# Top-k selection rounds spread over the attention's units, and the expert loop written out, in a float32 two-layer decoder trunk

## What is computed

```python
for l in range(2):
    # mixer: one input projection, two causal attentions, gates, output projection
    c_q, c_kv, k_r, dq, dk, dv, iq, ik, iw, gates = split_cols(x @ w_in[l])
    y_a = mla_branch(c_q, c_kv, k_r, pos, ...) @ w_o_mla[l]        # 8 heads
    y_b = dsa_branch(dq, dk, dv, iq, ik, iw, pos) @ w_o_dsa[l]     # 8 heads, 64 best keys per query
    g = sigmoid(gates)
    h = (g[..., :D] * y_a + g[..., D:] * y_b) @ w_out[l]
    x = layer_norm(ALPHA * x + h, ...)
    # layer 0: dense SwiGLU; layer 1: top-2 of 8 experts, D_FF_EXPERT = 3584
    x = layer_norm(ALPHA * x + (swiglu(x) if l == 0 else moe(x)), ...)
```

## Time and profile before

| | |
|---|---|
| median of 3 runs | 1639.26 us (1639.09 to 1640.32) |
| the profiled execution | 1640.06 us |
| its span in the trace | 1638.1 us |
| PE, DVE, ACT busy | 98%, 79%, 63% |
| attention of layer 0, of layer 1 | about 103 to 168 us, 503 to 568 us |
| expert jobs | 644 to 1626 us |
| mean granted TensorE clock | 0.989 of full speed |

### The profile page before, as it was taken

How to read it: one execution, slowest core, us unless ns; L and a number is a source line. 1 busy time by engine, 2 the same in 40 slices (tenths; PEclk the granted TensorE clock), 3 DMA queues, 4 the chain that set the end, 5 groups by cost and what they waited for, 6 DMA issues and landing times.

```text
span 1638.1 us, 20583 instructions
## 1 busy us (share of the span) xinstructions
PE 1601.2 (98%) x7637; PEld 1331.7 (81%) x7638; DVE 1292.3 (79%) x1298; ACT 1024.6 (63%) x947; POOL 55.9 (3%) x54
## 2 busy tenths in 40 slices
PE   8999999999999999999999999999999999999996
PEld 7888788888788788878888888888887888888885
DVE  6794675445697566888989888989888989888887
ACT  4655543443465643776777776777776777777773
POOL 0000000000000001000000200000200000200000
PEclk9999999999999998999999999999999999999998
DMA  9543366555453355899999998999998999999992
GB/s 313 182 146 116 105 217 206 192 187 187 134 172 129 103 181 189 308 357 323 364 376 366 367 373 310 369 375 365 357 375 317 370 375 364 369 372 335 364 371 88
DMA packets 230696, 453.23 MB, mean 277 GB/s; under 512 B 9920, under 2 KB 15552, under 8 KB 230592
## 3 DMA queue, kind: packets, MB, share of 16 engines
q1 hardware_dynamic: 228400, 447.60, 77.4%
q10 hardware_dynamic: 2192, 4.23, 0.7%
HBM read 450.75 MB, written 1.05 MB: 276 GB/s over the span
## 4 chain that ended last, share of the span: by engine, by line
PE 89%; DVE 7%; ACT 2%; issue 1%; DMA 0%; DVEq 0%; SPq 0%; ACTq 0%
PE bank L1515 27%; PE bank L1517 27%; PE bank L1516 27%; PE bank L1990 3%; DVE split L424 2%; PE bank L1685 1%; ACT split L418 1%; DVE split L440 1%; PE bank L1905 1%; ACT split L435 1%; PE bank L1876 0%; PE bank L1877 0%; PE bank L1714 0%; PE bank L1713 0%; DMA raw<-w_in_dram 0%
## 5 line engine op out<-in xcount | busy, mean ns | idle before, releaser
L440 DVE TENSOR_TENSOR split<-raw,split 128x2048 fp32r<-128x2048 f32 x327 | 747.4, 2289 | 110.7 <-ACT split L435 106.6
L435 ACT CAST split<-raw 128x2048 fp32r<-128x2048 f32 x327 | 625.6, 1914 | 188.8 <-PE bank L1517 188.8
L1515 PE MATMUL bank<-split,xe_pair 128*128 128x512 f32 x784 | 310.3, 396 | 3.8 <-DVE split L440 2.2
L1517 PE MATMUL bank<-split,xe_pair 128*128 128x512 f32 x784 | 305.9, 390 | 0.0
L1516 PE MATMUL bank<-split,xe_pair 128*128 128x512 f32 x784 | 305.3, 389 | 0.0
L424 DVE TENSOR_TENSOR split<-raw,split 128x2048 fp32r<-128x2048 f32 (+3 forms) x96 | 208.2, 2175 | 111.3 <-ACT split L418 111.0
L418 ACT CAST split<-raw 128x2048 fp32r<-128x2048 f32 (+3 forms) x96 | 174.3, 1818 | 169.2 <-PE bank L1517 169.2
L1515 PE MATMUL bank<-split,xT 128*128 128x512 f32 (+2 forms) x544 | 218.5, 402 | 4.5 <-DVE split L424 2.4
L1516 PE MATMUL bank<-split,xT 128*128 128x512 f32 (+2 forms) x544 | 209.3, 385 | 0.0
L1517 PE MATMUL bank<-split,xT 128*128 128x512 f32 (+2 forms) x544 | 209.2, 385 | 0.0
L1515 PE MATMUL bank<-split,hT 128*128 128x512 f32 x488 | 190.7, 391 | 0.0
(11 more groups left out here) (246 smaller groups left out, 1620.3 us busy)
## 6 DMA issues: line engine op xcount, KB each, us to landing
raw<-moe_w_dram SPq DMA_DIRECT2D x330, 1024.0 KB, 6.1
raw<-w_in_dram SPq DMA_DIRECT2D x31, 1024.0 KB, 5.1
raw<-dense_w_dram SPq DMA_DIRECT2D x30, 1024.0 KB, 5.0
raw<-w_out_dram SPq DMA_DIRECT2D x8, 1024.0 KB, 5.1
early<-moe_w_dram SPq DMA_DIRECT2D x6, 1024.0 KB, 12.6
raw<-w_o_mla_dram SPq DMA_DIRECT2D x4, 1024.0 KB, 5.1
raw<-w_o_dsa_dram SPq DMA_DIRECT2D x4, 1024.0 KB, 5.2
raw<-w_in_dram SPq DMA_DIRECT2D x4, 912.0 KB, 5.3
```

The costliest lines, as they stand in the source:

```text
L435: act.copy(split[:, n % SPLIT, HEAD, :], landing(n, j)[:, :]).then_inc(heads_made, 1)
L440: dve.tensor_tensor(split[:, n % SPLIT, REST, :], landing(n, j)[:, :], split[:, n % SPLIT, HEAD, :].bitcast(F32), ALU.subtract).then_inc(r ...
L1515: pe.matmul(out_, act_[REST], w[HEAD], start=first, stop=False)
L1517: return pe.matmul(out_, act_[HEAD], w[REST], start=False, stop=last)
```

## The change

In the attention (twice, once for each layer) DVE no longer does rounds 1 and 2 of `best_keys` and the rest of unit 16 ahead of `maxima(0)`. The rest of unit 16 comes behind `maxima(0)`, that of unit 17 behind `maxima(1)`, and one round of `best_keys` behind each of `maxima(0)` to `maxima(6)`; `selection()` follows `maxima(7)` instead of `maxima(6)`. The expert loop is emitted as straight code on all engines, with constants where registers stood. No arithmetic is added or left out.

```diff
         def all_jobs(eng, job):
 
             job(FIRST_JOB, "first")
-            with eng.Fori(1, EXPERTS - 1, 2) as j:
-                job((j, 0), "odd")
-                job((j, 1), "even")
+            for j in range(1, EXPERTS - 1):
+                job((j, 0), "odd" if j % 2 else "even")
             job((EXPERTS - 1, 0), "last")
...
             expert_stream(FIRST_JOB, 0)
-            with sp.Fori(1, EXPERTS - 1, 2) as e:
+            for e in range(1, EXPERTS):
                 expert_stream((e, 0), e)
-                expert_stream((e, 1), e + 1)
-            expert_stream((EXPERTS - 1, 0), EXPERTS - 1)
...
             pair_picks(FIRST_JOB, 1)
-            with pool.Fori(1, EXPERTS - 1, 2) as e:
+            for e in range(1, EXPERTS):
                 weights_of((e, 0), e)
-                weights_of((e, 1), e + 1)
-                pool.wait_ge(comb_tr, nth(1, (e, 1), 1 + CREDIT))
-                pair_picks((e, 1), e + 2)
-            weights_of((EXPERTS - 1, 0), EXPERTS - 1)
+                if e % 2 == 0:
+                    pool.wait_ge(comb_tr, nth(1, (e, 0), 1 + CREDIT))
+                    pair_picks((e, 0), e + 1)
...
                 keys_turned(1)
                 ropes_dsa(1, False)
                 rest(15)
-                rest(16)
-                best_keys(range(1, 3))
...
                 for u in range(16):
                     maxima(u)
-                    if u == 0:
-                        rest(17)
-                    if u < 5:
-                        best_keys(range(3 + u, 4 + u))
+                    if u < 2:
+                        rest(16 + u)
+                    if u < 7:
+                        best_keys(range(1 + u, 2 + u))
                     if u == 4:
                         rest(18)
-                    if u == 6:
+                    if u == 7:
                         selection()
                     if u == 7:
                         rest(19)
```

## The result

The changed kernel takes 1630.86 us, the median of 5 executions (1625.26 to 1631.29), against 1639.26 us before: a ratio of 0.9941, interval 0.9930 to 0.9953. In two later sets of executions it gave 0.9936 and 0.9956. It is faster, by 8.4 us between the medians where 7.9 were forecast (the ratio, which uses all executions, says 9.7, interval 7.7 to 11.5). The two numbers lie close together partly by luck: one term was missing, one came out larger, and the clock gave something that no term had.

What follows compares the result with a forecast made beforehand. PE, busy 98% of the span, was taken as the bound, so only its pauses could go: attention 4.2 plus loop 3.7 is 7.9 us, from 1639.26 to 1631.4 us. The range given was 1629.6 to 1634.8.

Steps and rivals of the forecast that it cites:

- Attention, 4.2 us: `qk(3)` no longer waits for `maxima(1)`, which has 1.5 us to spare; 2.1 us per layer, bounds 3.8 and 4.4.
- The loop, 3.7 us: Starts of jobs 3 and 5: PE's pauses of 1.8 and 1.9 us go, as at job 7.
- upper bound of 4.1: Most that the loop term was said to give; its lower bound was some 2.0 us.
- The rule on branches: Loop: a compare-and-branch costs about 108 ns, so two passes back are worth 0.2 us and the sum 4.4.
- The cost sits in going back: Jobs 3 and 5: the branch taken costs the pause, not the order of work; job 7, not taken, has none.
- I take no change: TensorE's clock behind each attention: same pauses, only earlier, so 0; a stretch more or less is worth 1.7 us.
- Attention gives nothing: Rival, chance 0.09: `maxima(1)` or `maxima(2)` misses its 1.5 us of cover; 1635.6 us, up to 1636.
- the loop gives only what a branch costs: Rival, chance 0.06: code comes late in straight line too, or DVE's order is the cause; 1634.9 us.
- More at half clock: Rival, chance 0.08: shifted pauses bring one or two stretches more, 1633.1 or 1634.8 us; one fewer gives 1629.7.
- more than one stretch: Sign that the forecast is wrong: more than one stretch at the lower clock comes or goes.
- The stalls of fresh straight code: Rival "Slower", chance 0.02: new code for jobs 3 to 6 stalls PE 16 times by 1.8 us; 1660 us.
- The forecast's own range: 1629.7 to 1633.3 us, from the bounds of both terms and one clock stretch; the forecast's chance was 0.72.

Runs made afterwards that it cites:

- experiments on single edits: Changed kernel with only the rests moved (rounds 1 and 2 as before), 1629.82 us; with only the rounds moved (rest of unit 16 as before), 1633.47 us.
- two instructions more: Changed kernel with rounds 1 and 2 ahead of `maxima(0)` as before and both rests moved; executes 19210 instructions in place of 19208; 1629.82 us.
- each half: Kernel before with the attention's edits alone, 1632.32 us (0.9965); changed kernel with the attention as before, so the loop written out alone, 1634.57 us (0.9976).
- padded: Changed kernel with 64 increments of an unused semaphore on DVE in layer 0; 1627.65 us, ratio 0.9927 to the kernel before.
- without the crowded code: Changed kernel without the code for experts with over 128 tokens and the jump over it; 1627.32 us, ratio 0.9926 to the kernel before.
- the last set: Changed kernel, unchanged, run again beside the kernel with 64 more DVE instructions; 1631.04 us, ratio 0.9956 to the kernel before.

## Why the prediction was right, and where it was not

**Attention, 4.2 us.** Right in mechanism: the pause, its cause, its cover (1.5 forecast, 1.7 seen) and the absence of a next one all came as said. From `qk(0)` to `qk(6)` the traces are 2.2 us shorter per layer, 4.3 in all. Half of the reason was idle, though: the text lets the two rounds and the rest go together, and the experiments on single edits show that the rest alone does it.

**The loop, 3.7 us.** The pauses went and jobs 3 and 5 start like job 7. The stage from job 1 to the last experts gave 4.2 to 4.3 us, a little over the upper bound of 4.1: the second matmul of the job was late too, by 0.1 us (1013.79 to 1014.12 in place of 0.23 apart). The engine that the term looked at was only half of it: DVE's own way back costs 3.2 us of stage by itself, hidden behind PE's 4.1. The rule on branches that would have left only 0.2 us (the Trainium skill, "Advanced Engine Details and Errata", Control Flow Timing, about 108 ns) is not borne out: PE idles 1.40 to 1.96 us per pass back, and the measurement decides.

**The step that failed** is that this term ended with the last job. "The cost sits in going back" was taken to mean that only the branches back cost. But straight code also moves everything behind it, and a jump forward at the very end now costs 2.09 us of issue in place of 0.48, 2.0 us in all, uncovered. The loop is thus worth 4.3 - 2.0 = 2.3 us and some 0.2 around the span (the time outside it is 1.72 in place of 1.95), in place of 3.7. The price of a jump whose target's code is late stood in the rows already, at jobs 3 and 5; what was missing was to ask which other jumps the edit would move. DVE's loop kept, jump left out, 64 instructions of padding and two instructions more each make the long pause vanish: this is shown.

**The other step that failed** is "I take no change" for the clock. Over all executions whose clock is on record, 16 of the changed kernel and 49 of the one before, the means are 1630.1 and 1639.2 us and the mean clocks 0.9906 and 0.9894 (each uncertain by 0.0003 or less). A straight line through the times of six kernels (changed, before, each half, padded, without the crowded code; 95 executions) gives 1.33 us per 0.001 of clock. So of the 9.1 us, 1.6 are clock, and at the same clock the changed kernel is 7.5 us faster, the attention alone 5.2, the loop alone 3.6 (standard errors 0.4). The traces account for 4.3 + 4.3 - 2.0 + 0.2 = 6.8 of the 7.5. For the halves they give 4.3 and 2.5, some 1 us less than measured in each, and the measured halves add up to 8.8, not 7.5; these gaps have no cause shown. By its time the loop's term would even seem right (3.6 against 3.7); that it is made of 4.3 and -2.0 is read from the traces. A part may lie ahead of the attention, in code that the change does not touch: with one stretch at the lower clock ahead of it, `qk(0)` starts at 102.80 us before, at 101.1 to 101.4 in seven profiles of the changed kernel and its variants, and near 103 again in two. The higher clock is in neither half (0.9899 each), only in both together, and in the last set it was 0.9902 (0.9895 before, beside it). That it belongs to the kernel is likely by the count of executions; why it does was not found.

**The rivals.** "Attention gives nothing" and "the loop gives only what a branch costs" are refuted by the two halves. "More at half clock" went the other way: its one stretch fewer, put at 1629.7, is near what came: the difference of 0.0012 in mean clock is about one stretch. The forecast had named "more than one stretch" coming or going as a sign that it is wrong, and the profiled execution has four fewer, a later one none fewer. The stalls of fresh straight code, feared inside jobs 3 to 6, are absent there; one of that kind appears behind job 7. The forecast's own range does not come out of its bounds either: 1639.26 less 4.4 and 4.1 is 1630.8, with one stretch fewer 1629.1, and less 3.8 and 2.0 it is 1633.5, where 1629.7 and 1633.3 were given.

## What to carry to other kernels

When a loop is written out, or any long piece of code grows or shrinks, check every jump behind it, above all the last one ahead of the kernel's end, where nothing covers a late instruction; a few instructions of padding can move it back. When several engines run the same loop, take the loop from all of them: what it costs on one can hide behind another. When an engine waits for a piece of work queued behind another engine's late one, move that one piece behind the urgent work and leave the rest. And where one kernel's executions differ by whole stretches of clock, compare two kernels at the same granted clock before giving a microsecond to an edit.

## What the runs showed of the hardware

- A forward jump over code that is not run cost DVE 0.48 us of issue in one layout and 2.09 in another, with the same instructions behind it; shifting the code by 64 instructions, or by two, changed 2.5 us of idle time to 0.57. In all seven profiles with the long pause a packet of DVE's instruction queue starts inside it, 2.0 to 2.1 us before DVE goes on; in the eight with the short one none does.
- A pass back costs each engine for itself: PE 1.40 to 1.96 us of idle time where PE loops, DVE up to 1.6 where DVE alone loops. Over two passes back the stage grows by 4.1 us with PE looping alone, 3.2 with DVE alone and 4.2 with all.
- 30 small matmuls in pauses of under 1 us behind the attentions kept the granted clock at 1.00 there in the three kernels that had them and cost some 2 us.
- Executions of one and the same kernel had three or seven stretches of 3.4 us at the lower clock and took 1625.3 and 1631.8 us. Short pauses behind the attention are answered by such a stretch in some executions and in others by none (0.66 and 1.00 at 166.7 us).
